# Prompt attention in a two-layer decoder step: row tiles from the last to the first, short rows grouped by heads, and two one-bank buffers for turning

## What is computed

```python
def blk(args):
    qi, bi = args
    s = jnp.einsum('bqhd,bkhd->bhqk', qi, k, preferred_element_type=F32)
    qpos = bi * qb_size + jnp.arange(qb_size)
    s = jnp.where(kpos[None, :] <= qpos[:, None], s, -jnp.inf)
    p = jax.nn.softmax(s, axis=-1)
    return jnp.einsum('bhqk,bkhd->bqhd', p.astype(v.dtype), v)
```

## Time and profile before

| | |
|---|---|
| time, median of 3 runs | 2188.83 us (2177.11 to 2195.06) |
| the profiled execution's own time | 2200.86 us |
| its span, from the first to the last instruction | 2199.1 us |
| busy share of the span: PE, PEld, DVE, ACT, POOL | 84%, 70%, 49%, 34%, 14% |
| mean granted TensorE clock | 0.904 |
| `prompt_attention`, first score to last copy | 601.1 to 842.8 us |

### The profile page before, as it was taken

The page is one execution under the profiler, slowest core; times in us unless marked ns, Lnnn a source line. Parts: engine busy times, 40 slices in busy tenths (PEclk is TensorE's granted clock), DMA queues, the critical chain, the costliest instruction groups (busy, mean ns, idle before and its releaser), DMA issues. The chain is left out here.

```text
span 2199.1 us, 30808 instructions
## 1 busy us (share of the span) xinstructions
PE 1843.8 (84%) x10530; PEld 1541.8 (70%) x10530; DVE 1080.7 (49%) x2054; ACT 752.1 (34%) x1590; POOL 306.8 (14%) x506
## 2 busy tenths in 40 slices
PE   4999994558789997799999899897597699999499
PEld 3977882335466774588888888886385588898387
DVE  4100103765565665366765765766322656556511
ACT  6212214214322221344444544443202354454400
POOL 1000000212300000222222222220000312221000
PEclk9999996779855987799999999999798699999699
DMA  4201110120000001231221231130223211110321
GB/s 127 68 20 29 41 46 27 21 70 10 13 31 1 1 1 41 72 89 39 63 74 47 55 85 46 50 84 1 99 96 106 71 28 37 43 43 21 128 79 56
DMA packets 128588, 113.09 MB, mean 51 GB/s; under 512 B 47665, under 2 KB 112002, under 8 KB 128322
## 3 DMA queue, kind: packets, MB, share of 16 engines
q1 hardware_dynamic: 128018, 111.14, 17.4%
q10 hardware_dynamic: 432, 0.20, 0.0%
HBM read 97.54 MB, written 13.76 MB: 51 GB/s over the span
## 5 line engine op out<-in xcount | busy, mean ns | idle before, releaser
L1449 PE MATMUL pg_k<-keys_queries,latents_high 128*128 128x288 f32 x2048 | 378.1, 306 | 0.0
L1449 PEld LDWEIGHTS pg_k<-keys_queries,latents_high 128*128 128x128 f32 x2048 | 297.2, 190 | 0.4 <-issue 0.4
L1563 DVE TENSOR_REDUCE ss<-sq_p 128x8 f32<-128x512 f32 x256 | 175.1, 684 | 174.8 <-ACT sq_p L1514 174.4
L1891 PE MATMUL rg_z<-x_odd_high,rg_w_parts 128*128 128x364 f32 (+1 forms) x960 | 242.8, 333 | 14.4 <-POOL rg_w_parts L188 14.4
L1514 ACT ACTIVATE sq_p<-pg_k 128x512 f32<-128x512 f32 x256 | 153.0, 598 | 241.0 <-PE pg_k L1449 241.0
L1449 PE MATMUL pg_k<-keys_queries,latents_low 128*128 128x288 f32 x1024 | 220.3, 296 | 0.0
L1891 PEld LDWEIGHTS rg_z<-x_odd_high,rg_w_parts 128*128 128x128 f32 x960 | 171.8, 190 | 16.3 <-issue 15.7
L1449 PEld LDWEIGHTS pg_k<-keys_queries,latents_low 128*128 128x128 f32 x1024 | 164.6, 189 | 0.0
L1891 PE MATMUL rg_z<-x_odd_low,rg_w_parts 128*128 128x364 f32 (+1 forms) x480 | 158.6, 330 | 0.0
L381 PE MATMUL pz<-w_even_high,x_even_high 128*128 128x512 f32 (+5 forms) x360 | 134.0, 372 | 10.2 <-DVE w_even_low L188 3.3
L1756 PE MATMUL out_py<-out_w_high,out_x_high 128*128 128x512 f32 x324 | 104.8, 406 | 44.3 <-DVE out_w_low L188 44.3
(11 more groups left out here) (345 smaller groups left out, 3315.8 us busy)
## 6 DMA issues: line engine op xcount, KB each, us to landing
cp<-in_cache_ckv SPq DMA_DIRECT2D x256, 128.0 KB, 2.0
w_even<-in_w_in_even SPq DMA_DIRECT2D x32, 256.0 KB, 2.6
wu<-in_w_in_odd SPq DMA_DIRECT2D x10, 512.0 KB, 4.0
wg<-in_w_in_odd SPq DMA_DIRECT2D x10, 512.0 KB, 4.9
out_w<-in_w_out_odd SPq DMA_DIRECT2D x10, 512.0 KB, 3.5
norm_xs<-in_x_p SPq DMA_DIRECT2D x8, 512.0 KB, 3.7
kr<-in_cache_kr SPq DMA_DIRECT2D x256, 16.0 KB, 1.8
out_w<-in_w_out_even SPq DMA_DIRECT2D x8, 512.0 KB, 3.5
```

The source lines that it names most:

```text
L1449: mm = pe.matmul(pk[p % 2][:, a, 0:WIDE + HQ // 2], w[:, p % CS, k, :], WQ[:, b % 2, k, s, a, :], start=(m == 0 and k == 0), stop=(m == 2 ...
L1563: dve.tensor_reduce(ss[:, p // NPG % 2, p % NPG, :], sq[:, p % 2, :, :], X, ALU.add).then_inc(summed, 1)
L1891: mm = pe.matmul(pz[z][:, j, 0:m], w[:, k, :], x[:, k, t0:t0 + m], start=(k == 0 and part == 0), stop=(k == KC - 1 and part == 2))
```

## The change

The units are built otherwise. Row tiles come from 7 down to 0, and a unit takes several heads where rows are short: eight for tile 0, four for tile 1, two for tiles 2 and 3, one for the others. There are 43 units instead of 64, the blocks of a unit are at most 8 as before, and `heads(n)` lays the heads side by side in the unit's score buffer. A unit has one mask instruction, one maximum and one reciprocal for all its heads, but still one exponential and one weighing for each.

`att_pt` becomes two buffers of one bank, four blocks each. A list, `order`, made before the engines' code, holds the uses of these buffers one after the other: the parts of a unit (up to four blocks) and the turning of `ob`. Use number `at` takes buffer `at % 2` and waits for the copy of use `at - 2` (`free`). A unit of more than four blocks has two turns and two copies. `turn_out` of a tile stands two units later than the tile's last unit, between that unit's turn and a value, and TensorE no longer waits behind it for ScalarE's copy; who takes the buffer next waits.

```diff
+    HEADS = (8, 4, 2, 2, 1, 1, 1, 1)
+    units = [(i, h) for i in reversed(range(PT)) for h in range(0, HM, HEADS[i])]
+    N = len(units)
+    blocks = [[(h + e, j) for e in range(HEADS[i]) for j in range(i + 1)] for i, h in units]
+    last_of = {i: n for n, (i, h) in enumerate(units)}
+    parts, order = [[] for _ in units], []
+    outs = {}
+    for n in range(N + 2):
+        if n < N:
+            for lo in range(0, len(blocks[n]), 4):
+                parts[n].append(len(order))
+                order.append((n, lo, min(lo + 4, len(blocks[n]))))
+        for i in range(PT):
+            if last_of[i] + 2 == n or (n == N + 1 and last_of[i] + 2 > n):
+                outs[i] = len(order)
+                order.append((i, None, None))
...
-        pt = c.ps(ctx, "att_pt", [P, PT, P])
+        pt = [c.ps(ctx, f"att_pt{i}", [P, 4, P]) for i in range(2)]
...
-        units = [(i, h) for i in range(PT) for h in range(HM)]
-        N = len(units)
+        def heads(n):
+            i, h = units[n]
+            stride = SEQ // HEADS[i]
+            return s[n % 2][:, :].rearrange("p (e w) -> p e w", w=stride)[:, :, 0:(i + 1) * P]
...
+                def free(at):
+                    if at >= 2:
+                        if order[at - 2][1] is None:
+                            pe.wait_ge(o_kept, o_before[at - 1])
+                        else:
+                            pe.wait_ge(t_kept, p_before[at - 1])
+
                 def turn(n):
-                    i, h = units[n]
                     pe.wait_ge(exped, n + 1)
-                    if n >= 1:
-                        pe.wait_ge(t_kept, n)
-                    for j in range(i + 1):
-                        mm = pe.transpose(pt[:, j, :], pr[:, n % 2, j * P:(j + 1) * P], c.ident[:, :])
-                    mm.then_inc(turned, 1)
+                    for at in parts[n]:
+                        free(at)
+                        _, lo, hi = order[at]
+                        for b in range(lo, hi):
+                            mm = pe.transpose(pt[at % 2][:, b - lo, :], pr[:, n % 2, b * P:(b + 1) * P], c.ident[:, :])
+                        mm.then_inc(turned, 1)
...
                 def turn_out(i):
-                    pe.wait_ge(weighed, HM * (i + 1))
-                    pe.wait_ge(t_kept, min(N, HM * (i + 1) + 1))
+                    pe.wait_ge(weighed, last_of[i] + 1)
+                    free(outs[i])
...
-                    pe.wait_ge(o_kept, i + 1)
 
                 score(0)
-                for n in range(N + 1):
+                for n in range(N + 2):
                     if n + 1 < N:
                         score(n + 1)
                     if n < N:
                         turn(n)
-                    if n >= 1:
+                    for i in reversed(range(PT)):
+                        if last_of[i] + 2 == n and n <= N:
+                            turn_out(i)
+                    if 1 <= n <= N:
                         value(n - 1)
-                        if n % HM == 0:
-                            turn_out(n // HM - 1)
+                turn_out(0)
...
+                    for e in range(HEADS[i]):
+                        m = i * HM + h + e
+                        ex = act.activation(pr[:, n % 2, e * L:(e + 1) * L], heads(n)[:, e, :], ACT.Exp, bias=mx[:, m:m + 1],
+                                            accum_out=den[:, m:m + 1])
...
+                        for at in parts[n]:
+                            _, lo, hi = order[at]
+                            dve.wait_ge(turned, p_before[at + 1])
+                            dve.tensor_copy(prT[:, n % 2, lo:hi, :], pt[at % 2][:, 0:hi - lo, :]).then_inc(t_kept, 1)
```

More of the change, by code:

```diff
@@ L18 @@
 from contextlib import ExitStack
+import itertools
 import numpy as np
@@ L1024, in prompt_attention @@
     nc = c.nc
+    HEADS = (8, 4, 2, 2, 1, 1, 1, 1)
[14 more added lines that the diff above has]
+                order.append((i, None, None))
+    p_before = list(itertools.accumulate((lo is not None for _, lo, _ in order), initial=0))
+    o_before = list(itertools.accumulate((lo is None for _, lo, _ in order), initial=0))
     with ExitStack() as ctx:
@@ L1052, in score @@
                         pe.wait_ge(exped, n - 1)
-                    length = (i + 1) * P
-                    for a in range(0, length, 512):
-                        w = min(512, length - a)
-                        mm = pe.matmul(s[n % 2][:, a:a + w], QT[:, h, cols(i)], KT[:, h, a:a + w], start=True, stop=True)
-                    mm.then_inc(scored, 1)
+                    for e in range(HEADS[i]):
+                        for a in range(0, (i + 1) * P, 512):
+                            w = min(512, (i + 1) * P - a)
+                            mm = pe.matmul(heads(n)[:, e, a:a + w], QT[:, h + e, cols(i)], KT[:, h + e, a:a + w],
+                                           start=True, stop=True)
@@ L1068, in value @@
                 def value(n):
                     i, h = units[n]
-                    pe.wait_ge(t_kept, n + 1)
                     if n >= 2:
                         pe.wait_ge(weighed, n - 1)
-                    for j in range(i + 1):
-                        mm = pe.matmul(po[n % 2][:, 0:VD], prT[:, n % 2, j, :], VB[:, j, h * VD:(h + 1) * VD],
-                                       start=(j == 0), stop=(j == i))
+                    for at in parts[n]:
+                        pe.wait_ge(t_kept, p_before[at + 1])
+                        _, lo, hi = order[at]
+                        for b in range(lo, hi):
+                            e, j = blocks[n][b]
+                            mm = pe.matmul(po[n % 2][:, (e - h) * VD:(e - h + 1) * VD], prT[:, n % 2, b, :],
+                                           VB[:, j, e * VD:(e + 1) * VD], start=(j == 0), stop=(j == i))
@@ L1130, in weigh @@
                     dve.wait_ge(valued, n + 1)
-                    step(dve, dve.reciprocal(den[:, n:n + 1], den[:, n:n + 1]))
-                    if i >= 2 and h == 0:
-                        dve.wait_ge(o_turned, i - 1)
-                    dve.scalar_tensor_tensor(out=ob[:, i % 2, h * VD:(h + 1) * VD], in0=po[n % 2][:, 0:VD],
-                                             scalar=den[:, n:n + 1], in1=gb[:, i, h * VD:(h + 1) * VD],
-                                             op0=ALU.mult, op1=ALU.mult).then_inc(weighed, 1)
+                    step(dve, dve.reciprocal(den[:, index(n)], den[:, index(n)]))
+                    if i < PT - 2 and h == 0:
+                        dve.wait_ge(o_turned, PT - i - 2)
+                    for e in range(HEADS[i]):
+                        at = slice((h + e) * VD, (h + e + 1) * VD)
+                        m = i * HM + h + e
+                        w = dve.scalar_tensor_tensor(out=ob[:, i % 2, at], in0=po[n % 2][:, e * VD:(e + 1) * VD],
+                                                     scalar=den[:, m:m + 1], in1=gb[:, i, at], op0=ALU.mult, op1=ALU.mult)
+                    w.then_inc(weighed, 1)
                 biggest(0)
@@ L1142, in _ @@
                     if n < N:
-                        i = units[n][0]
-                        dve.wait_ge(turned, n + 1)
                         if n >= 2:
                             dve.wait_ge(valued, n - 1)
-                        dve.tensor_copy(prT[:, n % 2, 0:i + 1, :], pt[:, 0:i + 1, :]).then_inc(t_kept, 1)
+                        for at in parts[n]:
+                            _, lo, hi = order[at]
+                            dve.wait_ge(turned, p_before[at + 1])
+                            dve.tensor_copy(prT[:, n % 2, lo:hi, :], pt[at % 2][:, 0:hi - lo, :]).then_inc(t_kept, 1)
                     if n >= 1:
```

35 lines of the change are left out of this document (20 added, 15 removed).

## The result

The changed kernel takes 2162.84 us, median (2155.07 to 2174.69), beside 2191.94 us of the kernel before (2177.11 to 2201.22) on the same chip: a ratio of 0.9869, interval 0.9827 to 0.9911. It is faster by 29 us. The forecast was 2140 us, 49 us faster, in a range of 2120 to 2162; the time lies 23 us above the forecast and 0.8 us outside the range. The sign was right, the size was not.

The account below looks back on a forecast made before the run. The prediction blamed the attention stage's 84 us above full-clock work, mostly low clock. Unit 39 at 757.2, tail 26, low clock 3.8 and 4 end it at 791, saving 52; 49 off the 2188.8 median gave 2140 us, range 2120 to 2162.

Parts of the forecast that it names:

- After that no wait over a fraction of a microsecond is left until the tail: Stage after the low-clock start: TensorE runs without longer waits until tiles 1 and 0, so the clock stays up.
- 757.2 + 3.8: End of the main body: unit 39, last of tile 2, turns at 757.2, plus 3.8 us of low clock.
- the 52: Whole program: saving of 52 us with everything as worked out, the stage ending at 791.
- 3.8 at the start: Start of the stage: TensorE begins at low clock after the load, losing 3.8 us, between 1.7 and 6.7.
- 26 + 4: Tiles 1 and 0, the last three units: 26 us of dependent chains plus 4 us of low clock (0 to 8).
- What would show it: Listed signs: tile 7 35 to 43 us, tiles 3 and 2 about 18 and 14, waits for `big` gone.
- the 84 us before: Old stage above 157.7 us of full-clock blocks: 9.4 waiting for `gb`, tile-end waits (7.0, 4.8), 47 low clock.
- (1): VectorE sets the pace in tiles 4, 2 and the tail: saving 40 us, 2149; chance 0.10.
- (2): Clock swings with the new buffers' waits, half of 264 blocks low: 2197 us, no change; chance 0.07.
- (3): Clock rises only after tile 7, eight units losing 33 us: saving 23, about 2167; chance 0.08.
- (4): Clock stays low throughout the stage: 77 us slower, 2266; chance 0.03.

Follow-up runs that it names:

- one short profile of before: The kernel before, unaltered, profiled in an execution of its shorter group: 2187.7 us, with an attention stage of 220.9 us.
- The late kernel: Changed kernel with TensorE turning a finished tile's `ob` behind the value, not ahead, and ScalarE copying it one exponential later: 2143.83 us, ratio 0.9748.
- the early mask: The late kernel with VectorE's first mask no longer waiting for the gates' load `gb`, only the first division: 2140.73 us, ratio 0.9763.

## Why the forecast was 23 us too low

The 23 us are two errors of about 14 and 9.

- **The stage, 14 us.** The forecast has it end at 791, 189.9 us long; the two profiles have 200.0 and 206.8. The step that failed: "The five turns of `ob` in between now stand before a value, with a copy by ScalarE that nothing waits for at once: only their 4 transposes count, 5 x 0.45 = 2.2." It asks who waits behind the turning and leaves out what the turning itself waits for. The use before last of its buffer is the first part of the unit just turned, whose copy stands on VectorE behind the next unit's maximum. The five waits are 8.4 us in both profiles (1.65, 1.62, 1.60, 1.81, 1.76), and the low clock behind two of them cost some 3.4 in the first. In the second it fell behind the last of them and stayed down for most of what was left. With them falls "After that no wait over a fraction of a microsecond is left until the tail". Unit 39 turns at 769.65, and at 773.60 in the second profile, and not at 757.2 + 3.8 = 761.0.
- **The baseline, 9 us.** "Against its own execution, 2200.9 - 52 = 2149; against the median, 2137", and 49 was taken. The profiled execution was one of those with the long stage, 241.7 us. By the one short profile of before, what it lay above the median was low clock in this stage. If so, the change takes that away in any case, so nearly all of the 12 us should have come off the 52. 189.9 us of stage, the rest of 1957.4 and the 1.8 between span and time give 2149, and with the 13.5 us that the stage came out longer (mean of the two) 2162.6; measured were 2162.84. That it comes so near is luck in part, as the rest of the program took between 1953.3 and 1965.1 us in the profiles. The text names the suspicion ("part of this may be more low clock in this very stage than usual") and prices it at 3 of 12.
- **What held.** The late kernel takes out the failed step and little else, and there the working comes out. Its unit 39 turns at 760.11, forecast 761.0. Its stage is 182.3 us; the forecast without loss in the tail and with 3.8 at the start is 783.2 + 3.8 - 601.1 = 185.9, and 22.2 us of tail measured against 26 are the difference. The price of a block at full clock, 0.5475 us, holds: between the two turnings around tile 6 the late kernel has 53 blocks of score, 54 of turning and 55 of value, 29.6 us, with 0.45 and a wait of 0.34 some 30.4, and takes 30.5.
- **The tail.** 30.8 us in the changed kernel's first profile for 26 + 4, with the last two windows at 0.59 and 0.50, and 34.8 in the second: the size was about right, by luck in part. It includes a sixth wait of 2.60 us that was not in the sum, and the late kernel, at full clock, shows that the 26 was too much. The longest idle time of TensorE was to stand before the last exponentials are turned; there it idled 1.45 us, and longest in that wait of 2.60.
- **What would show it.** Tile 7 with 41.8 us at 0.96 and tile 3 with 18.2 us came as listed, the waits for `big` are gone, and no second part of a turn waited for the copy. Tile 2 with 19.9 did not (about 14): the window holds the wait of 2.60 us and a stretch at 0.91.
- **Why it gains.** The text put most of the gain down to the clock, and that is right. Over the whole stage the mean granted clock is 0.75 in the profile before, 0.91 and 0.87 in the two after, and 0.96 in the late kernel. At 0.486 us lost of each low one that is an estimate of 59, 18, 26 and 7 us, and its differences are nearly the whole gain of the stage (42 and 35 us). But the text built the gain from the turned order, the groups and the buffers together. Any one of the three alone brings the stage to 205, 210 or 196 us, and they don't add up. What they share is that the clock comes up sooner in the short tiles, and each of them does that by itself. The account of the 84 us before was short as well: its three terms come to 68, and the low clock of tile 0 (0.50), for one, is in none of them. No term of the forecast rests on that.
- **Rivals.** (1), VectorE as the bound, fell with the late kernel. (2) fell as well: with the two one-bank buffers the clock stood at 1.00 from tile 1 to tile 7 in the old order (the late kernel), and alone they took 46 us off the longest stage of before. The forecast named a rule against this: the Trainium skill, "TensorE: Matmul & The Clock Gate", section "A second HAM failure mode: psum-queue depth-cycling", puts a swinging clock down to cycling through PSUM banks, by way of short pauses between groups of matmuls. The cycling alone brought no swinging in here. The pauses agree with the trace in part: behind a wait of 1.62 us a score took 2.87 us in one profile, and 1.51 behind the same wait in the next. (3) and (4) are refuted by tiles 7 and 6 at 0.96 and 1.00.

**What stays open.** Not every wait of 1.6 us brings the clock down: behind two of the five ahead of the tail it fell in the first profile of the changed kernel, behind one in the second, and behind none of four with the two buffers alone. What decides it, and why the last tiles run at 0.50 in one execution and at 1.00 in another, none of these runs tells. With tile 0 last, the late kernels had the tail at 1.00 in two of four profiles (0.67 in the last tile without groups, 0.57 with the early mask), and the kernels with `turn_out` in the old or the first place were low there in all four. So the late place may make the low tail rarer or shorter, and is not shown to exclude it.

The late kernel beats the changed one and the one before: 2143.83 us, ratio 0.9748, where the changed kernel beside it has 0.985.

## What to carry to other kernels

When a step is given a buffer of its own turn in a rotation, write down for it which use it evicts and where the copy of that use stands in its engine's order; if that copy lies behind other work, put independent work of the waiting engine ahead of it. When the clock of a stage runs differently from one execution to the next, take its gain from the new stage's length plus the rest of the program, and not as a difference from one profile carried over to the median. Where several edits each remove the same low-clock stretch, their gains don't add: price each alone. Here the best one alone took 46 us off the longest stage of before, and all three in the changed kernel 35 to 42.

## What the chip showed that I had not expected

- The clock of one kernel can take a few courses, and they repeat closely. The kernel before had stages of 241.7, 241.8 and 241.7 us, then 238.2 and 220.9; the turned order 205.2 and 205.1, with the same dips in the same tiles.
- Short units need not lose the clock. In the turned order tiles 3 to 1 ran at 1.00 with TensorE busy 18.51 of 20.10, 14.99 of 16.90 and 10.68 of 14.60 us; in the kernel before tile 2 stayed at 0.52 with TensorE busy 27.26 of 28.5 us. In those profiles a stretch that was reached with the clock up kept it, though TensorE idled more there; that is no rule, since it fell in tile 2 of the short execution of before and in tile 0 of the turned order.
- The start can matter for more than its own length: in the one profile where TensorE idled 0.46 us ahead of the first turn instead of 6.44, tile 7 ran at 1.00 instead of 0.93.
